# Squares of queries and keys in two fp32r parts: the sum over a head as two products with ones, behind the next tile's third quarter

## The chip, the cores and the metric

The kernel runs on one core of one Trainium2 chip. The metric is the device time in microseconds, lower is better. The engines are TensorE (PE, products), VectorE (DVE), ScalarE (ACT), GpSimd (POOL) and SyncE (SP, which starts transfers). Each works through its own queue in order, and they wait for one another by counting semaphores.

## The reference, cut to what matters

One layer of a hybrid encoder on 512 tokens of width 2048 in fp32: a combined input projection, three branches (banded attention, an RG-LRU, cross-attention into a memory), a gated merge, and a product-key expert layer. The change touches one spot: every query and key head of the banded attention is normed by the root mean square over its 128 numbers.

```
def rms_norm(x, g):
    y = xf * lax.rsqrt(jnp.mean(xf * xf, axis=-1, keepdims=True) + EPS)
    return (y * g.astype(jnp.float32)).astype(x.dtype)
...
h = rms_norm(x, norm1_g)
qa, ka, va, xl, gl, qc = jnp.split(h @ w_in, cuts, axis=-1)
qa = rms_norm(qa.reshape(B, S, A_HEADS, A_HEAD_DIM), attn_q_norm_g)
ka = rms_norm(ka.reshape(B, S, A_HEADS, A_HEAD_DIM), attn_k_norm_g)
...
log_a = -LRU_C * r * jax.nn.softplus(-lam)
a = jnp.exp(log_a)
mult = jnp.sqrt(jnp.clip(1.0 - jnp.exp(2.0 * log_a), 1e-12, 1.0))
u = mult * (i * xc)          # then an associative scan over the tokens
```

## The kernel before, in words

Activations lie transposed, features on the 128 partitions and the 512 tokens along the free axis. A weight tile is 2048x128 (16 blocks of 128x128); with it TensorE makes 128 output features for all tokens in one PSUM bank. fp32r is a form of fp32 with fewer bits that TensorE takes in one pass. To keep precision each product is made of three fp32r products (`split_mm`): high by high, high by low, low by high. The high part of a tile (`p_hi`) is a rounding copy on ScalarE (`high_part`), the low part (`p_lo`) a subtraction on POOL (`low_part`), and the two stand in single buffers that are refilled by quarters of four blocks: as soon as TensorE has used a quarter of one tile, that quarter of the next is rounded and subtracted. A tile is 48 products, a quarter is 12.

The stretch of the change is the sixteen tiles of queries and keys: loop `t` from 0 to 3 and `k` from 0 to 3, head 4t+k, tile into `bank[k]`. For each head, when its tile is done:

- ScalarE copies the bank to the arena, writes its square to `sq[k % 2]`, refills `p_hi`, and later takes the square root of the sum (`head_root`, which waits for `head_ss`).
- TensorE sums the square over the 128 partitions by one fp32 product with a 128x128 matrix of ones (`head_sum`, into bank 4 or 5). It does so in the middle of the *next* head's tile, behind its first quarter (`between` in `project_split`, `last_head`). The last head's product stands in the first tile of the values.
- VectorE takes the reciprocal of the root and scales the head (`head_norm`: a RECIPROCAL at L1218 and a SCALAR_TENSOR_TENSOR at L1220).

Written into the same loops is part of the RG-LRU branch. For t = 0 TensorE makes gate products behind the ones product, and ScalarE the sigmoids and tanh (`gate_pair`). For t = 1 VectorE computes the factors behind each head's norm (`lru_factors`, L1279 to L1285, seven instructions of 128x512, one of them a RECIPROCAL). For t = 2 ScalarE takes a root and VectorE does the scan (`lru_scan`, three instructions). All queues are written by hand; there is no scheduler. Buffers for the squares and roots are double, so ScalarE waits for the ones product of head k-2 before it writes a square, and for the norm of head k-2 before it writes a root.

Of the kernel before, what the change touches and what calls it, by code (L numbers as in the profile page):

```python
# [158 lines left out]
def hybrid_block(nc, x_t, mem_t, g1, g2, gmem, head_g, w_memk, w_memv, w_qk, w_lru_in, w_v, rel_rev,  # L159
                 lru_w, lru_vec, w_mix, b_gate, w_o, w_pq, keys, w_exp, u_rows, v_rows, out_t):  # L160
    ctx = ExitStack()
    with ctx:
# [109 lines left out]
        ig = at(XL, LC, S)  # L272
        la = at(Z + 2048, LC, S)
        lr = at(TZ + 1536, S)
        fill_sq = [place(f"fill_sq{i}", 199.0625 + 2 * i, [S]) for i in range(2)]

        tb = at(TZ, HA, 2 * P)
# [115 lines left out]
        wg_in, act_raw = [sem(f"wg_in{i}") for i in range(2)], [sem(f"act_raw{i}") for i in range(2)]  # L393
        u_gelu, act_part, act_ok, y_added = sem("u_gelu"), sem("act_part"), sem("act_ok"), sem("y_added")
        out_done = sem("out_done")
        wait_held, pool_held = sem("wait_held"), sem("pool_held")
        dve_step, pool_step = sem("dve_step"), sem("pool_step")

        def band_s(e, q):
# [222 lines left out]
        def _(pool):  # L622
# [126 lines left out]
            def gather(first, rows, index, t, following=None):  # L749
                for b in range(4):  # L750

                    pool.wait_ge(gath_col, 4 * t + b + 1 + first)
                    for half in range(2):
                        to = 2 * (b % 2) + half
                        pool.wait_ge(gath_free, 8 * t + 2 * b + half + 1 + 2 * first)  # L755
                        pool.sem_inc(pool_held, 1)
                        pool.indirect_dma_start(grow[to][:, :], None, rows,  # L757
                                                bass.IndirectOffsetOnAxis(g_col[b][:, half:half + 1], 0)).then_inc(gath_in[to], 16)
                    if following is None or b < 2:
                        column(index, 4 * t + b + 2, (b + 2) % 4)  # L760
                    else:
                        column(following, b - 2, b - 2)
# [26 lines left out]
        def _(act_e):  # L789
# [107 lines left out]
            for t in range(N_QK // 4):  # L897
                for k in range(4):
                    act_e.wait_ge(tile_done, 4 * t + T_QK + k + 1)
                    f(head_place(t, k), bank[k][:, :]).then_inc(acc_copied, 1)  # L900
                    act_e.wait_ge(head_ss, 4 * t + k + HC - 1)
                    f(sq[k % 2], bank[k][:, :], ACT.Square).then_inc(head_sq, 1)
                    ahead = (k % 2, 4 * t + S_QK + k + 2, 2 * t + S_QK // 2 + k // 2 + 2, 4 * t + T_QK + k + 2)
                    high_part(*ahead, quarters=(0,))
                    act_e.wait_ge(head_ok, 4 * t + k + HC - 1)
                    head_root(k, S, 4 * t + k + HC + 1)
                    if t == 0:
                        gate_pair(k)
                    if t == 2:
                        act_e.wait_ge(lru_m2, k + 1)  # L910
                        f(rg[:, k, :], rg[:, k, :], ACT.Sqrt).then_inc(lru_mult, 1)
                    high_part(*ahead, quarters=(1, 2, 3))

            act_e.wait_ge(lru_ok, LC)
            act_e.wait_ge(rel_out, 16)
# [263 lines left out]
        def _(dve):  # L1179
# [107 lines left out]
            def lru_scan(k):  # L1287
# [5 lines left out]
                v.tensor_tensor_scan(out=gl[:, k, :], data0=la[:, k, :], data1=u, initial=0.0, op0=ALU.mult, op1=ALU.add  # L1293
                                     ).then_inc(lru_ok, 1)

            dve.wait_ge(conv_ok, LC)

            for t in range(N_QK // 4):
                for k in range(4):
                    head_norm(k, head_place(t, k), S, hgain[:, t // 2:t // 2 + 1], 4 * t + k + HC + 1)  # L1300
                    if t == 1:
                        lru_factors(k)
                    if t == 2:
                        lru_scan(k)
# [159 lines left out]
            def best16(groups):  # L1464

                def pause():
                    st.wait()
                    dve.sem_inc(wait_held, 1)

                dve.sem_inc(wait_held, 1)  # L1470
                for half in (slice(0, 8), slice(8, 16)):
                    for s, val, idx in groups:
                        st.did(v.max(val[:, half], s))
                    pause()
                    for s, val, idx in groups:
                        st.did(v.max_index(idx[:, half], val[:, half], s))
                    pause()
                    if half.start == 0:
                        for s, val, idx in groups:
                            st.did(v.match_replace(s, val[:, half], s, LOWEST))  # L1480
                        pause()
# [282 lines left out]
        def _(pe):  # L1764
# [60 lines left out]
            def project_split(number, out, r_hi, r_lo, between=None):  # L1825

                for q in range(4):
                    pe.wait_ge(quarter_lo, 4 * number + q + 1)
                    for c in range(4 * q, 4 * q + 4):
                        ins = split_mm(out, p_hi[:, c, :], p_lo[:, c, :], r_hi[:, c, :], r_lo[:, c, :], c == 0, c == KC - 1)  # L1830
                    ins.then_inc(part_used if q < 3 else tile_done, 1)
                    if q == 0 and between is not None:
                        between()


# [19 lines left out]
            def last_head(t, k):  # L1855

                pe.wait_ge(head_rt, 4 * t + k + HC - 2)
                head_sum((k - 1) % 4, S, 4 * t + k + HC)

            def with_gates(t, k):  # L1860
                if t or k:
# [17 lines left out]
            for half in range(2):  # L1879
                if half:  # L1880
                    pe.wait_ge(head_rt, HC + N_QK)
                for n in range(4):
                    wh, wl = (w[:, :, :].rearrange("p (c a) b -> p c (a b)", c=4) for w in (p_hi, p_lo))
                    for c in range(4):
# [5 lines left out]
                            ins = split_mm(bank[4 * half + m][:, :], norm_hi[:, 4 * n + c, tok], norm_lo[:, 4 * n + c, tok],  # L1890
                                           wh[:, c, :], wl[:, c, :], n == 0 and c == 0, n == 3 and c == 3)
                        ins.then_inc(part_used if c < 3 else tile_done, 1)
                        if half == 0 and n == 0 and c == 0:
                            last_head(N_QK // 4, 0)


# [374 lines left out]
```

## Time and profile before

| | us |
|---|---|
| median of 3 runs | 3813.01 (3811.71 to 3814.02) |
| the profiled execution's own time | 3809.69 |
| its span | 3807.9 |
| TensorE busy | 3759.3 (99%) |
| VectorE busy | 2364.7 (62%) |
| ScalarE busy | 1262.9 (33%) |
| POOL busy | 1702.0 (45%) |

Matmuls overlap in the records: one fp32r product of 512 columns is recorded with 0.39 us, while the next starts 0.23 us later. So the cost of a product is read from the distance of the starts, not from its duration. An fp32 product appears as two records (x2). In a timeline the bracket at the end of a row tells how long the engine was idle before it and who ended that.

### The profile page before, as it was taken

Reading aid. Unit: us, or ns where it says so; the run is one execution under the profiler, and the core shown is the slowest. Engines: PE = TensorE matmul, PEld = TensorE weight load, DVE = VectorE, ACT = ScalarE, POOL = GpSimd, SP = SyncE. Lnnn points to the kernel's source line nnn. Section 1 sums busy time; section 2 is a strip of 40 time slices with the busy share of each in tenths; the row PEclk is TensorE's granted clock in tenths of the full one; section 3 lists DMA queues with packets and bytes.
Section 4 is the critical chain, followed back from the end, with each engine's and each line's share of the span. In section 5 each row is a group of like instructions: output and inputs, shape, how many; then the busy total and the mean of one; then the engine's idle time right before and its main releaser. Section 6 shows DMA issues by size and latency. Waiting matters only on the chain. (4 is left out here: it accounts for less than half of the span.)

```text
span 3807.9 us, 56597 instructions
## 1 busy us (share of the span) xinstructions
PE 3759.3 (99%) x20173; PEld 3446.9 (91%) x20173; DVE 2364.7 (62%) x4027; ACT 1262.9 (33%) x1638; POOL 1702.0 (45%) x1449
## 2 busy tenths in 40 slices
PE   7999999999999998999999999999999999999999
PEld 5778778888888887889999999999999999999999
DVE  5482453000010207886968888888887888888887
ACT  3433453333333323224652222222222222222221
POOL 0444334444444662444015555545553655554223
PEclk9999999999999999999999999999999999999999
DMA  6222112222222322334569998899987898889787
GB/s 205 92 88 100 67 58 98 99 92 95 99 99 92 140 99 104 105 105 151 211 247 330 326 332 318 322 326 334 322 313 281 319 339 311 316 320 340 275 295 249
DMA packets 187946, 800.97 MB, mean 210 GB/s; under 512 B 21024, under 2 KB 59944, under 8 KB 134440
## 3 DMA queue, kind: packets, MB, share of 16 engines
q1 hardware_dynamic: 99776, 492.34, 35.8%
q0 software_dynamic: 83872, 303.22, 22.4%
q10 hardware_dynamic: 4184, 4.01, 0.5%
q8 instruction: 56, 0.92, 0.1%
q14 instruction: 58, 0.48, 0.0%
HBM read 762.39 MB, written 37.09 MB: 210 GB/s over the span
## 5 line engine op out<-in xcount | busy, mean ns | idle before, releaser
L791 ACT ACTIVATE w_hi<-ring 128x1024 fp32r<-128x1024 f32 (+1 forms) x499 | 564.0, 1135 | 1090.1 <-PE bank L1766 718.8
L637 POOL TENSOR_TENSOR p_lo<-ring,p_hi 128x512 fp32r<-128x512 f32 x432 | 563.9, 1306 | 672.5 <-ACT p_hi L791 672.5
L1766 PE MATMUL bank<-h_hi,w_hi 128*128 128x368 f32 (+1 forms) x2304 | 780.3, 339 | 13.1 <-DVE h_lo L1449 7.3
L1766 PE MATMUL bank<-h_lo,w_hi 128*128 128x368 f32 (+1 forms) x2304 | 773.9, 336 | 0.0
L1766 PE MATMUL bank<-h_hi,w_lo 128*128 128x368 f32 (+1 forms) x2304 | 773.7, 336 | 0.0
L1766 PE MATMUL bank<-act_hi,w_hi 128*128 128x368 f32 x2048 | 673.1, 329 | 0.3 <-DVE xT L1640 0.3
L1766 PE MATMUL bank<-act_hi,w_lo 128*128 128x368 f32 x2048 | 672.8, 329 | 0.0
L1766 PE MATMUL bank<-act_lo,w_hi 128*128 128x368 f32 x2048 | 672.8, 328 | 0.0
L757 POOL DMA_INDIRECT grow<-v_rows,g_col x288 | 382.2, 1327 | 516.3 <-DVE g_acc L1621 389.9
L1586 DVE TENSOR_TENSOR w_lo<-ring,w_hi 128x1024 fp32r<-128x1024 f32 x448 | 546.2, 1220 | 77.3 <-ACT w_hi L791 56.6
L791 ACT ACTIVATE p_hi<-ring 128x512 fp32r<-128x512 f32 x464 | 292.7, 632 | 788.7 <-PE bank L1766 784.2
L757 POOL DMA_INDIRECT grow<-u_rows,g_col x288 | 376.0, 1305 | 387.1 <-DVE grow L1614 308.1
L1766 PE MATMUL bank<-norm_hi,p_hi 128*128 128x512 f32 x1216 | 487.0, 400 | 1.7 <-POOL p_lo L637 1.7
L1766 PE MATMUL bank<-norm_hi,p_lo 128*128 128x512 f32 x1216 | 473.7, 390 | 0.0
L1766 PE MATMUL bank<-norm_lo,p_hi 128*128 128x512 f32 x1216 | 473.3, 389 | 0.0
L1766 PEld LDWEIGHTS bank<-h_hi,w_hi 128*128 128x128 f32 x2304 | 433.6, 188 | 25.7 <-issue 8.7
L1766 PEld LDWEIGHTS bank<-h_lo,w_hi 128*128 128x128 f32 x2304 | 433.6, 188 | 9.8
L1766 PEld LDWEIGHTS bank<-h_hi,w_lo 128*128 128x128 f32 x2304 | 433.2, 188 | 10.2
L1393 DVE TENSOR_TENSOR arena<-arena,bank 128x512 f32<-128x512 f32 x48 | 30.1, 683 | 572.4 <-PE bank L1766 572.4
L1766 PEld LDWEIGHTS bank<-act_hi,w_hi 128*128 128x128 f32 x2048 | 384.1, 188 | 1.2 <-DVE xT L1640 1.2
L1766 PEld LDWEIGHTS bank<-act_lo,w_hi 128*128 128x128 f32 x2048 | 384.1, 188 | 0.0
L1766 PEld LDWEIGHTS bank<-act_hi,w_lo 128*128 128x128 f32 x2048 | 384.1, 188 | 0.0
(219 smaller groups left out, 5056.3 us busy)
## 6 DMA issues: line engine op xcount, KB each, us to landing
ring<-w_exp SPq DMA_DIRECT2D x256, 1024.0 KB
ring<-w_mix SPq DMA_DIRECT2D x64, 1024.0 KB, 4.9
tables<-wt SPq DMA_DIRECT2D x12, 2048.0 KB, 6.8
wg<-tables SPq DMA_DIRECT2D x96, 256.0 KB
ring<-w_qk SPq DMA_DIRECT2D x20, 1024.0 KB, 4.9
ring<-w_o SPq DMA_DIRECT2D x16, 1024.0 KB, 4.9
ring<-w_pq SPq DMA_DIRECT2D x16, 1024.0 KB
xT<-x_t SPq DMA_DIRECT2D x8, 1024.0 KB, 11.9
```

What stands on the lines that cost most here:

```text
L637: nc.gpsimd.tensor_tensor(p_lo[:, part, :], ring[slot][:, part, :], p_hi[:, part, :].bitcast(F32), ALU.subtract).then_inc(quarter_lo, 1)
L757: pool.indirect_dma_start(grow[to][:, :], None, rows, bass.IndirectOffsetOnAxis(g_col[b][:, half:half + 1], 0)).then_inc(gath_in[to], 16)
L791: return nc.scalar.activation(out, in_, func, **kw)
L1393: v.tensor_tensor(sig[:, b, :], sig[:, b, :], bank[3 + b][:, :], ALU.mult).then_inc(y_used, 1)
L1586: v.tensor_tensor(w_lo[b][:, part, :], ring[b][:, part, :], w_hi[b][:, part, :].bitcast(F32), ALU.subtract).then_inc(split_lo, 1)
L1766: return nc.tensor.matmul(out, lhsT, rhs, start=start, stop=stop)
```

## The change: what it does

- ScalarE rounds each square once more, to `sq_hi` (fp32r); VectorE subtracts it from the square, to `sq_lo` (fp32r), which lies where the square lay. `ones_r` is an fp32r copy of the ones, made once.
- TensorE's fp32 ones product of a head becomes two fp32r products into the same bank, ones by `sq_hi` and ones by `sq_lo`. They wait for a new counter, `head_lo`, that VectorE raises with each subtraction, instead of for ScalarE's square.
- The products (with the gate products where there are any) stand behind the third quarter of the next tile instead of behind its first; on ScalarE the root and what follows it stand behind the next tile's third p_hi quarter.
- The subtraction stands at the head of a head's round on VectorE, before its norm.
- Two counters that only mark held instructions become one.

```diff
@@ ScalarE
                     f(sq[k % 2], bank[k][:, :], ACT.Square).then_inc(head_sq, 1)
+                    act_e.wait_ge(head_sq, 4 * t + k + HC + 1)
+                    f(sq_hi[k % 2][:, :], sq[k % 2]).then_inc(h_high, 1)
                     ahead = (k % 2, 4 * t + S_QK + k + 2, 2 * t + S_QK // 2 + k // 2 + 2, 4 * t + T_QK + k + 2)
-                    high_part(*ahead, quarters=(0,))
+                    high_part(*ahead, quarters=(0, 1, 2))
                     act_e.wait_ge(head_ok, 4 * t + k + HC - 1)
                     head_root(k, S, 4 * t + k + HC + 1)
...
-                    high_part(*ahead, quarters=(1, 2, 3))
+                    high_part(*ahead, quarters=(3,))
@@ VectorE
+            v.tensor_copy(ones_r[:, :], ones[:, :]).then_inc(head_lo, 1)
             dve.wait_ge(conv_ok, LC)

             for t in range(N_QK // 4):
                 for k in range(4):
+                    dve.wait_ge(h_high, KC + 4 * t + k + 1)
+                    v.tensor_tensor(sq_lo[k % 2][:, :], sq[k % 2], sq_hi[k % 2][:, :].bitcast(F32), ALU.subtract
+                                    ).then_inc(head_lo, 1)
                     head_norm(k, head_place(t, k), S, hgain[:, t // 2:t // 2 + 1], 4 * t + k + HC + 1)
@@ TensorE
-                    if q == 0 and between is not None:
+                    if q == 2 and between is not None:
                         between()
...
             def last_head(t, k):

                 pe.wait_ge(head_rt, 4 * t + k + HC - 2)
-                head_sum((k - 1) % 4, S, 4 * t + k + HC)
+                n = (k - 1) % 2
+                pe.wait_ge(head_lo, 4 * t + k + 1)
+                mm(bank[4 + n][:, :], ones_r[:, :], sq_hi[n][:, :], start=True, stop=False)
+                mm(bank[4 + n][:, :], ones_r[:, :], sq_lo[n][:, :], start=False, stop=True).then_inc(head_ss, 1)
...
-                        if half == 0 and n == 0 and c == 0:
+                        if half == 0 and n == 0 and c == 2:
                             last_head(N_QK // 4, 0)
```

How the instructions stand in the queues is shown at two places; the code lines of the changed kernel lie a few lines lower. First VectorE's queue before, from the norm of head 4 (t = 1, k = 0; `hgain` is the head's gain, `head_rt` counts ScalarE's roots) through the RG-LRU factors to the norm of head 5:

```order
L1218 RECIPROCAL arena<-arena 128x512 [waits head_rt]
L1220 SCALAR_TENSOR_TENSOR arena<-arena,hgain 128x512 [waits dve_step]
L1279 TENSOR_SCALAR arena<-arena 128x512 [waits lru_tanh]
L1280 RECIPROCAL arena<-arena 128x512 [waits dve_step]
L1281 TENSOR_SCALAR arena<-arena 128x512 [waits dve_step]
L1282 TENSOR_TENSOR arena<-arena 128x512 [waits dve_step]
L1283 SCALAR_TENSOR_TENSOR arena<-arena 128x512 [waits dve_step]
L1284 TENSOR_TENSOR arena<-arena 128x512 [waits dve_step]
L1285 TENSOR_SCALAR arena<-arena 128x512 [waits dve_step]
L1218 RECIPROCAL arena<-arena 128x512 [waits head_rt]
```

And the same stretch of it now, where `sq_hi_121` and `sq_lo_123` are the two parts of head 5's square:

```order
L1225 RECIPROCAL arena<-arena 128x512 [waits head_rt]
L1227 SCALAR_TENSOR_TENSOR arena<-arena,hgain 128x512 [waits dve_step]
L1286 TENSOR_SCALAR arena<-arena 128x512 [waits lru_tanh]
L1287 RECIPROCAL arena<-arena 128x512 [waits dve_step]
L1288 TENSOR_SCALAR arena<-arena 128x512 [waits dve_step]
L1289 TENSOR_TENSOR arena<-arena 128x512 [waits dve_step]
L1290 SCALAR_TENSOR_TENSOR arena<-arena 128x512 [waits dve_step]
L1291 TENSOR_TENSOR arena<-arena 128x512 [waits dve_step]
L1292 TENSOR_SCALAR arena<-arena 128x512 [waits dve_step]
L1309 TENSOR_TENSOR sq_lo_123<-arena,sq_hi_121 128x512 [waits h_high]
L1225 RECIPROCAL arena<-arena 128x512 [waits head_rt]
```

The subtraction of head 5 stands behind the norm and the factors of head 4, and ahead of head 5's own norm.

Next ScalarE's queue before, in the round of a head of t = 1 (copy, square, then `p_hi` by quarters, with the root in between, which alone reads `eps`):

```order
L791 ACTIVATE arena<-bank 128x512 [waits tile_done]
L791 ACTIVATE arena<-bank 128x512 [waits head_ss]
L791 ACTIVATE p_hi<-ring_52 128x512 [waits part_used,pair_in1]
L791 ACTIVATE arena<-bank,eps 128x512 [waits head_ss,head_ok]
L791 ACTIVATE p_hi<-ring_52 128x512 [waits part_used,pair_in1]
L791 ACTIVATE p_hi<-ring_52 128x512 [waits part_used]
L791 ACTIVATE p_hi<-ring_52 128x512 [waits tile_done]
```

And now:

```order
L796 ACTIVATE arena<-bank 128x512 [waits tile_done]
L796 ACTIVATE arena<-bank 128x512 [waits head_ss]
L796 ACTIVATE sq_hi_121<-arena 128x512 [waits head_sq]
L796 ACTIVATE p_hi<-ring_52 128x512 [waits part_used,pair_in1]
L796 ACTIVATE p_hi<-ring_52 128x512 [waits part_used] x2
L796 ACTIVATE arena<-bank,eps 128x512 [waits head_ss,head_ok]
L796 ACTIVATE p_hi<-ring_52 128x512 [waits tile_done,pair_in1]
```

The root has moved behind two more quarters of p_hi, and the rounding of the square is new, ahead of them all.

## Rows read from the trace of the kernel before

**Rows 1.** The page's first part: busy us, share of the span, instructions.
```profile
PE 3759.3 (99%) x20173; PEld 3446.9 (91%) x20173; DVE 2364.7 (62%) x4027; ACT 1262.9 (33%) x1638; POOL 1702.0 (45%) x1449
```

**Rows 2.** Windows: busy us (instructions) of PE, PEld, DVE, ACT, POOL; PEclk, DMA share, GB/s.
```profile
200.00:240.00 40.00, 40.00 (x171) 31.86 (x170) 36.84 (x27) 15.39 (x25) 17.95 (x14) 1.00 0.29 105
240.00:280.00 40.00, 40.00 (x173) 32.01 (x172) 38.17 (x25) 15.50 (x27) 18.80 (x15) 1.00 0.22 79
320.00:360.00 40.00, 40.00 (x176) 32.73 (x176) 8.55 (x5) 10.58 (x18) 18.10 (x14) 1.00 0.33 115
```

**Rows 3.** Waits of PE from 60 to 620 us: total us, times, longest us.
```profile
PE bank L1766 <- POOL p_lo L637: 1.7, 1, 1.7
...
```

**Rows 4.** Timeline of PE: start us, us, engine, instruction, count.
```profile
293.57 1.02 PE L1766 MATMUL bank<-arena,ones 128*128 128x512 f32 x2
...
294.65 0.39 PE L1766 MATMUL bank<-norm_lo,p_hi 128*128 128x512 f32 x1
...
305.35 1.02 PE L1766 MATMUL bank<-arena,ones 128*128 128x512 f32 x2
```

**Rows 5.** Timeline of ACT: heads 1 and 12, same columns.
```profile
159.99 1.28 ACT L791 ACT_TABLE_LOAD   x1 [0.21 <-PE bank L1766]
...
165.67 0.62 ACT L791 ACTIVATE p_hi<-ring 128x512 fp32r<-128x512 f32 x1
...
294.68 0.69 ACT L791 ACTIVATE arena<-bank,eps 128x512 f32<-128x512 f32 x1 [0.23 <-PE bank L1766]
```

**Rows 6.** Timeline of DVE in the head tiles.
```profile
202.44 3.35 DVE L1218 RECIPROCAL arena<-arena 128x512 f32<-128x512 f32 x1 [8.47 <-ACT arena L791]
...
212.36 1.68 DVE L1284 TENSOR_TENSOR arena<-arena 128x512 f32<-128x512 f32 x1
...
214.41 3.35 DVE L1218 RECIPROCAL arena<-arena 128x512 f32<-128x512 f32 x1
...
223.87 1.83 DVE L1282 TENSOR_TENSOR arena<-arena 128x512 f32<-128x512 f32 x1
...
227.52 3.35 DVE L1218 RECIPROCAL arena<-arena 128x512 f32<-128x512 f32 x1
...
240.75 3.34 DVE L1218 RECIPROCAL arena<-arena 128x512 f32<-128x512 f32 x1
...
253.68 3.35 DVE L1218 RECIPROCAL arena<-arena 128x512 f32<-128x512 f32 x1
...
261.75 3.32 DVE L1218 RECIPROCAL arena<-arena 128x512 f32<-128x512 f32 x1
...
271.84 3.35 DVE L1218 RECIPROCAL arena<-arena 128x512 f32<-128x512 f32 x1 [1.27 <-ACT arena L791]
...
295.40 3.35 DVE L1218 RECIPROCAL arena<-arena 128x512 f32<-128x512 f32 x1 [3.63 <-ACT arena L791]
```

**Rows 7.** Timeline of POOL in the head tiles.
```profile
212.07 1.41 POOL L637 TENSOR_TENSOR p_lo<-ring,p_hi 128x512 fp32r<-128x512 f32 x1 [1.48 <-ACT p_hi L791]
...
223.85 1.29 POOL L637 TENSOR_TENSOR p_lo<-ring,p_hi 128x512 fp32r<-128x512 f32 x1 [1.48 <-ACT p_hi L791]
```

**Rows 8.** Two tiles, norm_hi and norm_lo: ns min/median/max, first and last start.
```profile
L791 ACT ACTIVATE norm_hi<-hT x16: 629/630/634, 62.9 to 81.4; 128x512 fp32r<-128x512 f32 x16
```
...
L1242 DVE TENSOR_TENSOR norm_lo<-hT,norm_hi x16: 671/674/693, 63.6 to 82.0; 128x512 fp32r<-128x512 f32 x16
```

**Rows 9.** Timeline of DVE and PE behind the merge: h_lo, and the product behind it.
```profile
1448.62 0.69 DVE L1449 TENSOR_TENSOR h_lo<-arena,h_hi 128x512 fp32r<-128x512 f32 x1
...
1449.45 0.76 PE L1766 MATMUL bank<-h_hi,w_hi 128*128 128x512 f32 x1 [7.29 <-DVE h_lo L1449]
```

**Rows 10.** Windows near the start (columns as in rows 2), and PE's timeline.
```profile
22.00:23.00 1.00, 0.00 (x0) 0.00 (x0) 0.96 (x3) 1.00 (x2) 0.00 (x0) 0.76 1.02 397
...
25.00:26.00 1.00, 1.00 (x4) 0.82 (x3) 1.00 (x3) 1.00 (x2) 0.00 (x0) 0.54 1.04 422
...
23.07 1.19 PE L1766 MATMUL bank<-arena,ring 128*128 128x256 f32 x2 [4.38 <-DVE arena L1202]
```

More of the change, by code:

```diff
@@ L274, in hybrid_block @@
         lr = at(TZ + 1536, S)
+        sq_hi = [nc.alloc_sbuf_tensor_at(f"sq_hi{i}", [P, S], F32R, offset=base + 96 * 1024 + 4 * (QC + 512 * i))
+                 for i in range(2)]
+        sq_lo = [nc.alloc_sbuf_tensor_at(f"sq_lo{i}", [P, S], F32R, offset=base + 96 * 1024 + 4 * (Z + 1024 * i + 512))
+                 for i in range(2)]
+        ones_r = place("ones_r", 203.0625, [P], F32R)
         fill_sq = [place(f"fill_sq{i}", 199.0625 + 2 * i, [S]) for i in range(2)]
@@ L395, in hybrid_block @@
         out_done = sem("out_done")
-        wait_held, pool_held = sem("wait_held"), sem("pool_held")
+        held, head_lo = sem("held"), sem("head_lo")
         dve_step, pool_step = sem("dve_step"), sem("pool_step")
@@ L755, in gather @@
                         pool.wait_ge(gath_free, 8 * t + 2 * b + half + 1 + 2 * first)
-                        pool.sem_inc(pool_held, 1)
+                        pool.sem_inc(held, 1)
                         pool.indirect_dma_start(grow[to][:, :], None, rows,
@@ L1467, in pause @@
                     st.wait()
-                    dve.sem_inc(wait_held, 1)
-                dve.sem_inc(wait_held, 1)
+                    dve.sem_inc(held, 1)
+                dve.sem_inc(held, 1)
                 for half in (slice(0, 8), slice(8, 16)):
```

## The prediction

> **What bounds the kernel now.** I read the page's busy times first: TensorE is busy 99% of the span [rows 1]. The reader is to see that little but TensorE work or a TensorE wait can move the end. Then the stretch that the change touches, the 16 head tiles from about 134 to 329 us, by windows [rows 2]: TensorE shows no idle time and its clock is granted in full, but VectorE is busy 36.8 and 38.2 of 40 us between 200 and 280 us, against 8.6 of 40 later. That second figure is the one to keep. The waits of TensorE from 60 to 620 us [rows 3] are three, of which the longest is 1.7 us: its queue runs from product to product, and nothing in the stretch is there to be won back but the products themselves. Last I read the timelines of the engines for single rounds.
>
> **What the ones products cost and what replaces them.** In a late tile [rows 4] the ordinary products go from 294.65 to 305.35 us in 47 steps, 0.2277 us each. From the start of the fp32 ones product (293.57) to 294.65 lie that product and one ordinary one: 1.08 - 0.23 = 0.85 us. From one ones product to the next is 11.78 us, the round of a head. The change puts two fp32r products of 512 columns there, which the stream prices at 2 x 0.2277 = 0.455 us. Gain 0.40 us a head, 16 heads: -6.4 us. Bounds: if each new product cost its whole record of 0.39 us, only 0.07 us a head would go (-1.1 us); if the second, which has the same weights as the first, cost next to nothing, 0.63 us (-10 us). I take -6.4, since the stream around it consists of such products. A round without waits becomes 11.38 us.
>
> **What is added beside TensorE.** ScalarE gets 16 roundings of 0.63 us [rows 8]; it is busy 15.5 of 40 us, so they cost nothing. In the first four heads it also does root, gates and table loads, which now come behind the third quarter: from the load at 159.99 to the next p_hi at 165.67 are 5.7 us [rows 5], after which the fourth quarter's p_hi (0.63) and p_lo (1.3) follow. The load starts 0.7 us after the ones product does, the tile ends 4.9 us after it (0.455, two fp32 gate products of 0.85, a quarter of 2.73), so this p_lo is ready 3.5 us into the next tile, which wants it after three quarters (8.2 us). Covered by 4.7 us; beyond that it would cost the excess, four times. The last tile's product goes behind the third quarter of the first V tile, and the last head's norm comes 5 us later; POOL asks for it many V tiles on. The merged counter of held indirect loads and the single copy of the ones cost nothing that I can see. The quarters of p_hi that are moved ahead of the root have no row that waits for the root.
>
> **The term that decides: the low part stands in VectorE's queue.** Each head gets a subtraction of 128x512 with fp32r output, 0.67 us alone [rows 8]. It stands at the head of the next round, so *behind* the norm and the RG-LRU factors of the head before. And TensorE now waits for it (head_lo); before it waited only for ScalarE's square. So in heads 4 to 7 a closed loop arises: ones product of head k-1, root, reciprocal, norm, seven factor instructions, subtraction of head k, ones product of head k. Its length, from rows:
> - ones product to root 1.11 us, root to reciprocal 0.72 us [rows 4 to 6]; less the 0.40 that the product is shorter: 1.43.
> - reciprocal to reciprocal through norm and factors: the first begins at 202.44, the fifth at 253.68, none of the five waiting in between [rows 6]: 51.24 / 4 = 12.81.
> - subtraction: 0.72 with its gap; it reads two operands in the arena beside POOL's p_lo and can be held as other such instructions are. L1284 took 1.68 instead of some 0.7 us with a p_lo begun at 212.07, L1282 1.83 with one begun at 223.85 [rows 6, 7]. The round of 11.97 us has one such case of 0.99 and a small one of 0.10, so the bare round is 10.88, and the mean holds 1.93 us of collisions over seven exposed instructions, 0.28 each. Subtraction 1.0.
> - from VectorE's end to TensorE's start 0.14 (1449.31 to 1449.45) [rows 9].
>
> Sum 15.4 us against a round of 11.38: TensorE stands 4.0 us, before the products of heads 5, 6, 7 and 8, each time anew, since the loop starts from the delayed product. Behind the waiting product stand the fourth quarter of its tile and everything that follows on TensorE. 4 x 4.0 = +16.0 us. The first loop has a table load (1.28, as at 159.99) ahead of its root; part of it is lost against a p_lo that would hold the same instruction anyway: +0.6.
>
> Bounds of a stall: without any collision 1.43 + 10.88 + 0.72 + 0.14 - 11.38 = 1.8 us; with the worst round seen (13.23, from four rounds) and a held subtraction (1.83) 5.2 us. So +7.2 to +21 for the four.
>
> The Trainium skill (SBUF — State Buffer, section "SBUF: two separate sides") says that VectorE and GpSimd hold their shared port pair exclusively for a whole instruction, a VectorE instruction with two SBUF inputs included, and that the other fully blocks. The rows of 1.68 and 1.83 us beside a p_lo agree. By that rule the collisions stay in the loop, 4.0 us a stall; if the ports were merely split evenly, the stall would lie nearer to 1.8 us.
>
> In heads 8 to 11 the three scan instructions stand in the loop instead: reciprocal to reciprocal 8.07 us at 253.68 to 261.75, and 8.8 us (10.09 less 1.27 idle) at 261.75 to 271.84 [rows 6]. With 1.43, 0.72 to 1.83 and 0.14 the loop is 10.4 to 12.2 against 11.38: 0 to 0.8 us a head; I take +0.2 in all. In the other eight heads it is 1.43 + 4.1 + 1.0 and never decides.
>
> **The clock.** After 4.38 us of idle before 23.07 us the granted clock was 0.76 in the window 22 to 23 and 0.50 until 25 to 26 (0.54) [rows 10]: it fell to the level of 1.2 GHz some 4.1 us after TensorE's last product and cost about 1.4 us (2.9 us at half speed). A stall of 4.0 us lies just at that edge. A fall in a stall whose loop follows costs only the longer ones product (0.45 us), for the loop is otherwise made of VectorE work and the slower tile merely shortens the next stall; only behind the last stall would the 1.4 us count in full. Between 0 and 3.2 us; I take +0.7.
> The Trainium skill (TensorE: Matmul & The Clock Gate, section "What's actually happening") has it that throttled is the default state and only activity releases it; were all four stalls long enough, its rule would give the full 3.2 us, which makes rival 3.
>
> **Sum.** -6.4 + 16.0 + 0.6 + 0.2 + 0.7 = +11.1 us. Against the profiled execution's 3809.7 us (span 3807.9 and 1.8 around it) that is 3820.8; the median of the runs is 3813.0, 3.3 higher, and the change adds the same to it: **3824**. The delay passes through whole: later stages start from TensorE's queue.
>
> **Rivals.**
> 1. *No stall (3806.6).* The place is the product of head 5. If the subtraction were done by then, only the -6.4 us would stand. It decides from where the loop is under 11.38 us. For it: TensorE was never held by VectorE here before [rows 3]. Against it: the bare loop of 13.2 us is longer, and rounds of VectorE alone took 12.81 us. Chance 4%.
> 2. *Short stalls (3814 to 3819).* The pause of TensorE also pauses ScalarE and POOL, so fewer p_lo fall on factor instructions; with stalls of 1.8 to 2.8 us the sum is -6.4 + 7.2 to 11.2, or +0.8 to +4.8, and with a little clock and scan up to +6. For it: between two stalls POOL makes four p_lo in 15.4 instead of 11.78 us. Against it: each p_lo follows its tile quarter at a fixed distance, so the same instructions are hit every round. 14%.
> 3. *Long stalls and a fallen clock (3830 to 3837).* Stalls near 5.2 us, or the clock down after each, scan rounds held: -6.4 + 21 + 3.2 + 2, at most +20; from about +17 on I count it here. For it: the 4.1 us edge. Against it: a fall shortens the following stall. 12%.
> 4. *Faster by over 0.2% (3805 and less).* Needs no stall and the cheap second product, -10 us. 1%.
>
> The forecast itself, 3819 to 3830, has 69%.
>
> **How the numbers follow.** A measurement tells about 0.2%, 7.6 us, from no change. Faster: 1 to 2%. Within 0.2% (3805.4 to 3820.6): rivals 1 and 2 and the low edge of the forecast, 0.04 + 0.14 + 0.02 = 0.20. Slower: the rest, 0.78. Range for 8 in 10: 3815.5 to 3831, which leaves out rival 1, the lower end of 2 and the upper half of 3; both ends are of one sign.
>
> **What would show it.** In the profile after: TensorE waits for the subtraction's line four times, some 4 us each, longest between 205 and 270 us, and nowhere else in the head tiles; two ones products with 0.23 us steps; rounds of 11.38 us in heads 12 to 15 and of 15.4 us in heads 5 to 8; VectorE without idle time in heads 4 to 7; the granted clock at or just below full there. I am wrong if TensorE has no wait there, if ScalarE's fourth-quarter p_hi is late in heads 0 to 3 (TensorE waiting for p_lo), or if the time lost is seen in a stage behind the head tiles.

## The result, and the profile after

| | before | after |
|---|---|---|
| median of 7 runs, us | 3811.89 (3808.34 to 3814.04) | 3824.83 (3819.64 to 3827.48) |
| ratio, 95% interval | | 1.0027 [1.0018, 1.0036] |
| span of the profiled execution | 3807.9 | 3824.1 |
| head 0's ones product to the first product behind the merge | 1298.6 | 1308.7 |

By the ratio the changed kernel is slower by 10.3 us (6.9 to 13.7); the medians lie 12.9 us apart. The last line of the table is the measure that I use throughout, and I call it the stretch: it is read from one trace and holds no noise of the later gathers. It begins with head 0's ones product, behind the third quarter of the next tile. In the kernel before that product stands behind the first quarter, at 145.41 us, so its stretch is counted from two quarters later, 24 steps of 0.2277 us: from 150.87 to 1449.45 [rows 9]. After, it runs from 151.23 to 1459.97: +10.1 us, so the whole loss was made before the merge, and the waits below put it into the head tiles. The two spans differ by 16.2; of the rest, 3.8 us are waits of TensorE for the low part of a weight tile behind gathers (7.6 against 3.8 us from 1470 us on), a thing that varies from run to run (3.1 us in e5, 9.7 in e7); the last 2 us I have not traced.

Busy times of the page, against rows 1. TensorE is busy as long as before in a longer span:

```profile
PE 3759.9 (98%) x20173; PEld 3451.9 (90%) x20173; DVE 2374.5 (62%) x4044; ACT 1272.4 (33%) x1654; POOL 1701.2 (44%) x1449
```

The windows of rows 2 again (PE, PEld, DVE, ACT, POOL busy; granted clock; DMA):

```profile
200.00:240.00 40.00, 34.74 (x141) 27.87 (x140) 29.24 (x22) 14.73 (x24) 15.40 (x12) 0.91 0.20 75
240.00:280.00 40.00, 34.77 (x142) 27.94 (x141) 32.97 (x26) 13.55 (x23) 15.74 (x12) 0.91 0.24 79
320.00:360.00 40.00, 40.00 (x177) 32.92 (x176) 15.37 (x9) 14.15 (x24) 18.12 (x14) 1.00 0.33 113
```

TensorE now has 10.5 us without work in 80, and the clock is not full. VectorE, the engine that is waited for, is *less* busy there than before (29.2 and 33.0 against 36.8 and 38.2 us). An engine in a closed loop waits itself for a part of each round; its busy share does not show that it is the bound. The waits do. TensorE's, 60 to 620 us (total us, times, longest), against rows 3:

```profile
PE bank L1777 <- DVE sq_lo L1309: 10.5, 4, 4.0
PE bank L1777 <- POOL p_lo L642: 1.7, 1, 1.7
```

Four waits, all for the subtraction. The products of heads 4 to 9 on TensorE's timeline, with those of 12 (against rows 4):

```profile
203.55 0.40 PE L1777 MATMUL bank<-sq_hi,ones_r 128*128 128x512 f32 x1
203.78 0.39 PE L1777 MATMUL bank<-sq_lo,ones_r 128*128 128x512 f32 x1
...
219.06 0.77 PE L1777 MATMUL bank<-sq_hi,ones_r 128*128 128x512 f32 x1 [3.96 <-DVE sq_lo L1309]
...
234.55 0.47 PE L1777 MATMUL bank<-sq_hi,ones_r 128*128 128x512 f32 x1 [1.30 <-DVE sq_lo L1309]
...
250.11 0.77 PE L1777 MATMUL bank<-sq_hi,ones_r 128*128 128x512 f32 x1 [3.93 <-DVE sq_lo L1309]
...
265.43 0.47 PE L1777 MATMUL bank<-sq_hi,ones_r 128*128 128x512 f32 x1 [1.30 <-DVE sq_lo L1309]
...
276.85 0.40 PE L1777 MATMUL bank<-sq_hi,ones_r 128*128 128x512 f32 x1
...
311.03 0.40 PE L1777 MATMUL bank<-sq_hi,ones_r 128*128 128x512 f32 x1
```

From start to start: 15.51, 15.49, 15.56, 15.32 us, then 11.42 and on to 311.03 in three rounds of 11.39. The waits alternate, 3.96 and 1.30, but the rounds do not: behind a long wait the clock is down, the tile's products take longer, and the next wait is shorter by that much. So the loss is not the waits (10.5 us) but what the four rounds are longer: 61.88 against 4 x 11.39 = 45.56, or 16.3 us.

The loop in VectorE's timeline, head 4's norm to head 5's:

```profile
206.41 3.35 DVE L1225 RECIPROCAL arena<-arena 128x512 f32<-128x512 f32 x1 [7.50 <-ACT arena L796]
...
216.22 1.63 DVE L1291 TENSOR_TENSOR arena<-arena 128x512 f32<-128x512 f32 x1
217.89 0.43 DVE L1292 TENSOR_SCALAR arena<-arena 128x512 f32<-128x512 f32 x1
218.23 0.68 DVE L1309 TENSOR_TENSOR sq_lo<-arena,sq_hi 128x512 fp32r<-128x512 f32 x1
221.07 3.35 DVE L1225 RECIPROCAL arena<-arena 128x512 f32<-128x512 f32 x1 [2.16 <-ACT arena L796]
```

The subtraction ends at 218.91 and TensorE starts at 219.06. VectorE then waits 2.16 us for the root that hangs on this very product: that idle bracket is the closed loop. L1291 took 1.63 us beside the p_lo that began at 215.84, as L1284 did before [rows 6].

And the clock, by windows of 1 us (columns as in rows 2):

```profile
217.00:218.00 1.00, 0.00 (x0) 0.00 (x0) 0.96 (x2) 0.00 (x0) 0.31 (x1) 0.88 0.00 0
218.00:219.00 1.00, 0.00 (x0) 0.00 (x0) 0.91 (x2) 0.00 (x0) 0.00 (x0) 0.50 0.00 0
...
223.00:224.00 1.00, 1.00 (x4) 0.77 (x3) 1.00 (x1) 0.00 (x0) 0.00 (x0) 0.50 0.00 0
224.00:225.00 1.00, 1.00 (x5) 0.82 (x4) 0.96 (x2) 0.00 (x0) 0.00 (x0) 0.70 0.00 0
```

TensorE's last product before the wait ended at 215.10. The clock fell at about 217.8 to the 1.2 GHz level and came back at about 224.6, so 5.5 us of work ran at half speed; behind the second long wait it was 5.2.

### The profile page after: what moved, and what is told of

It is laid out like the page before. It is cut to its first block, busy times and chain, and to the rows that moved or that the text cites. A ratio compares the mean times of both kernels' runs of the same rounds, so it can differ in the third digit from the quotient of the medians.

```text
span 3824.1 us, 56630 instructions
## 1 busy us (share of the span) xinstructions
PE 3759.9 (98%) x20173; PEld 3451.9 (90%) x20173; DVE 2374.5 (62%) x4044; ACT 1272.4 (33%) x1654; POOL 1701.2 (44%) x1449
## 4 chain that ended last, share of the span: by engine, by line
PE 85%; issue 7%; DMA 3%; DVE 3%; POOL 1%; ACT 1%; ACTq 0%; POOLq 0%; DVEq 0%
PE bank L1777 85%; DMA grow<-v_rows,g_col 2%; DMA grow<-u_rows,g_col 1%; POOL grow L762 1%; DVE arena L1287 0%; DVE arena L1225 0%; DVE w_lo L1597 0%; DVE g_acc L1632 0%; PE bank L1939 0%; ACT w_hi L796 0%; POOL g_col L752 0%; DVE arena L1291 0%; ACT arena L796 0%; POOL w_lo L733 0%; DVE xT L1651 0%
## 5 line engine op out<-in xcount | busy, mean ns | idle before, releaser
L796 ACT ACTIVATE w_hi<-ring 128x1024 fp32r<-128x1024 f32 (+1 forms) x499 | 564.2, 1136 | 1113.4 <-PE bank L1777 711.9
L642 POOL TENSOR_TENSOR p_lo<-ring,p_hi 128x512 fp32r<-128x512 f32 x432 | 566.0, 1311 | 681.0 <-ACT p_hi L796 681.0
L1777 PE MATMUL bank<-h_hi,w_hi 128*128 128x368 f32 (+1 forms) x2304 | 781.5, 339 | 17.1 <-DVE w_lo L1597 7.6
L1777 PE MATMUL bank<-h_lo,w_hi 128*128 128x368 f32 (+1 forms) x2304 | 775.4, 337 | 0.0
L1777 PE MATMUL bank<-h_hi,w_lo 128*128 128x368 f32 (+1 forms) x2304 | 775.0, 336 | 0.0
L1777 PE MATMUL bank<-act_hi,w_hi 128*128 128x368 f32 x2048 | 672.8, 328 | 0.0
L1777 PE MATMUL bank<-act_lo,w_hi 128*128 128x368 f32 x2048 | 672.8, 328 | 0.0
L1777 PE MATMUL bank<-act_hi,w_lo 128*128 128x368 f32 x2048 | 672.8, 328 | 0.0
L796 ACT ACTIVATE p_hi<-ring 128x512 fp32r<-128x512 f32 x464 | 292.6, 632 | 780.7 <-PE bank L1777 776.4
L1777 PE MATMUL bank<-norm_hi,p_hi 128*128 128x512 f32 x1216 | 484.2, 398 | 1.7 <-POOL p_lo L642 1.7
L1777 PE MATMUL bank<-norm_hi,p_lo 128*128 128x512 f32 x1216 | 475.1, 391 | 0.0
L1777 PE MATMUL bank<-norm_lo,p_hi 128*128 128x512 f32 x1216 | 475.0, 391 | 0.0
L1777 PEld LDWEIGHTS bank<-h_hi,w_hi 128*128 128x128 f32 x2304 | 434.6, 189 | 29.8 <-DVE w_lo L1597 9.0
L1777 PEld LDWEIGHTS bank<-h_hi,w_lo 128*128 128x128 f32 x2304 | 434.3, 188 | 10.2
L1777 PEld LDWEIGHTS bank<-h_lo,w_hi 128*128 128x128 f32 x2304 | 434.6, 189 | 9.9
L1777 PEld LDWEIGHTS bank<-act_hi,w_hi 128*128 128x128 f32 x2048 | 384.1, 188 | 0.0
L1777 PEld LDWEIGHTS bank<-act_lo,w_hi 128*128 128x128 f32 x2048 | 384.1, 188 | 0.0
L1777 PEld LDWEIGHTS bank<-act_hi,w_lo 128*128 128x128 f32 x2048 | 384.1, 188 | 0.0
```

What stands on the lines that cost most here:

```text
L642: nc.gpsimd.tensor_tensor(p_lo[:, part, :], ring[slot][:, part, :], p_hi[:, part, :].bitcast(F32), ALU.subtract).then_inc(quarter_lo, 1)
L796: return nc.scalar.activation(out, in_, func, **kw)
L1777: return nc.tensor.matmul(out, lhsT, rhs, start=start, stop=stop)
```

## The experiments

"Stretch" is the last line of the table above, against 1298.6 us before; for e5 it starts two quarters behind the beginning of its first wait. Ratios are to the kernel before on the same chip.

| kernel | stretch | ratio, 95% interval |
|---|---|---|
| after | +10.1 | 1.0027 [1.0018, 1.0036] |
| e1_pool_sub | -6.2 | 0.9975 [0.9963, 0.9987] |
| e2_high_only | -10.2 | 0.9978 [0.9969, 0.9987] |
| e3_square_wait | 0.0 | 1.0002 [0.9993, 1.0012] |
| e4_no_recip | -2.0 | 0.9995 [0.9986, 1.0004] |
| e5_first_quarter | +17.1 | 1.0044 [1.0031, 1.0057] |
| e6_place_only | 0.0 | 1.0006 [0.9997, 1.0015] |
| e7_sub_first | +4.4 | 1.0013 [1.0004, 1.0021] |
| e8_more_recip | +22.7 | 1.0064 [1.0052, 1.0076] |
| e9_keep_busy | +10.3 | 1.0030 [1.0021, 1.0040] |

The theory is the closed loop; the rivals are that the added work, the new place, a low part wherever it is made, or the fallen clock costs the time.

### e1: the subtraction on POOL

```diff
@@ VectorE
-                    dve.wait_ge(h_high, KC + 4 * t + k + 1)
-                    v.tensor_tensor(sq_lo[k % 2][:, :], sq[k % 2], sq_hi[k % 2][:, :].bitcast(F32), ALU.subtract
-                                    ).then_inc(head_lo, 1)
@@ POOL, behind low_part of tile `number` (the tile ahead)
+                pool.wait_ge(h_high, KC + number - S_QK)
+                nc.gpsimd.tensor_tensor(sq_lo[n][:, :], sq[n], sq_hi[n][:, :].bitcast(F32), ALU.subtract
+                                        ).then_inc(head_lo, 1)
```

> The subtraction of each square's low part is done by POOL, behind the fourth p_lo quarter of the tile ahead, instead of standing in VectorE's queue; all else as in the changed kernel. Theory (the loop through VectorE's factors holds TensorE): TensorE waits nowhere in the head tiles, rounds are 11.4 us from head 4 on, and only the shorter products are left: 6.4 us under the kernel before, ratio 0.9983 (3805.5 us where before has 3812). VectorE's rounds with factors go back to about 12.8 us. Rival (any product that waits for a low part is late, wherever it is made, or the fp32r pair and its place cost the time): ratio 1.002 to 1.003, TensorE still held four times. Rival (POOL becomes the late one): TensorE waits for p_lo or for the subtraction by up to 1 us a head, ratio 0.999 to 1.002.

TensorE has no wait for a low part of a square left; these are its waits from 60 to 620 us, two products of the former loop, and POOL's subtraction for head 8:

```profile
PE bank L1795 <- POOL p_lo L642: 1.7, 1, 1.7
PE bank L1795 <- DVE arena L1361: 1.6, 1, 1.6
PE bank L1795 <- DVE mix_lo_c L1415: 0.2, 1, 0.2
```

```profile
215.14 0.40 PE L1795 MATMUL bank<-sq_hi,ones_r 128*128 128x512 f32 x1
...
226.53 0.40 PE L1795 MATMUL bank<-sq_hi,ones_r 128*128 128x512 f32 x1
```

```profile
243.76 1.29 POOL L650 TENSOR_TENSOR sq_lo<-arena,sq_hi 128x512 fp32r<-128x512 f32 x1 [0.34 <-ACT sq_hi L817]
245.01 1.47 POOL L642 TENSOR_TENSOR p_lo<-ring,p_hi 128x512 fp32r<-128x512 f32 x1
```

Rounds are 11.39 us from head 4 on. POOL's next p_lo begins where the subtraction ends, and TensorE waits for neither. The stretch is 6.2 us shorter than before. This is also the version that beats both kernels, by its interval 5 to 14 us under the one before. One expectation missed: VectorE's rounds did not go back to 12.8 us, they take 14.3 ((263.85 - 206.61) / 4), because POOL now has a fifth instruction a head that can hold VectorE: an instruction of 0.69 us (L1312) took 1.67 at 233.04, beside the POOL subtraction of a square that began at 232.42. Nobody waits for these rounds.

### e2: the high part alone

```diff
-                pe.wait_ge(head_lo, 4 * t + k + 1)
-                mm(bank[4 + n][:, :], ones_r[:, :], sq_hi[n][:, :], start=True, stop=False)
-                mm(bank[4 + n][:, :], ones_r[:, :], sq_lo[n][:, :], start=False, stop=True).then_inc(head_ss, 1)
+                pe.wait_ge(head_lo, 1)
+                pe.wait_ge(h_high, KC + 4 * t + k)
+                mm(bank[4 + n][:, :], ones_r[:, :], sq_hi[n][:, :]).then_inc(head_ss, 1)
```
(and the subtraction removed)

> The low part is left out: one fp32r product of ones by the rounded square, which waits for ScalarE's rounding alone (the sums lose the low parts). Theory: no wait in the head tiles, and 0.855 less 0.228 us a head are saved, 16 heads: 10.0 us under the kernel before, ratio 0.9974. If a fp32r product of ones costs more than the step of the stream around it, the ratio lies between 0.9974 and 0.9983. Rival (rounding on ScalarE or the later place costs the 10 to 12 us): ratio 1.001 or more.

Stretch -10.2, rounds of 11.13 us (214.87 to 226.00), no wait for a square. The price list holds to a few hundredths: beside 48 steps of 0.2277 us (10.93) the round of 11.78 leaves 0.85 us for the fp32 product, that of 11.13 leaves 0.20 for one fp32r product, and that of 11.39 leaves 0.46 for two. The ratio's interval (0.9969 to 0.9987) includes 0.9974.

### e3: all the work, without the wait

```diff
-                pe.wait_ge(head_lo, 4 * t + k + 1)
-                mm(bank[4 + n][:, :], ones_r[:, :], sq_hi[n][:, :], start=True, stop=False)
-                mm(bank[4 + n][:, :], ones_r[:, :], sq_lo[n][:, :], start=False, stop=True).then_inc(head_ss, 1)
+                head_sum((k - 1) % 4, S, 4 * t + k + HC)
@@ sq_lo in a buffer of its own; ScalarE, before the square
+                    if 4 * t + k > 1:
+                        act_e.wait_ge(head_lo, 4 * t + k)
```

> All the added work and the new places stay (rounding, subtraction at the head of VectorE's round, third quarter), but TensorE does the old fp32 product on the square and waits for ScalarE's square alone; the low part is made beside it and read by nobody. Theory (the wait is what costs, not the work): no wait in the head tiles, rounds of 11.78 us, ratio 1.0000 +- 0.0005; VectorE's rounds with factors 13.5 to 14 us, and nobody waits for them. Rival (the added VectorE or ScalarE work or the later root costs): ratio 1.002 to 1.003 with TensorE waiting for p_lo or a root.

Stretch 0.0. VectorE has the same subtraction in the same place, and gets later with each head, but TensorE waits for the square alone:

```profile
221.09 0.69 DVE L1311 TENSOR_TENSOR sq_lo<-arena,sq_hi 128x512 fp32r<-128x512 f32 x1
...
235.65 0.68 DVE L1311 TENSOR_TENSOR sq_lo<-arena,sq_hi 128x512 fp32r<-128x512 f32 x1
...
250.15 0.68 DVE L1311 TENSOR_TENSOR sq_lo<-arena,sq_hi 128x512 fp32r<-128x512 f32 x1
```

14.5 us a round, where 13.5 to 14 had been expected, against 11.78 of TensorE. TensorE is not held by it: the work costs nothing, only the wait for it does.

### e4: a shorter loop, and e8: a longer one

```diff
@@ e4, lru_factors
-                step(v.reciprocal(lr, lr))
@@ e8, lru_factors
                 step(v.reciprocal(lr, lr))
+                step(v.reciprocal(spare_r, rt[k % 2]))
```

> The changed kernel, with the reciprocal left out of the RG-LRU factors (that output is computed otherwise). It takes 3.39 us out of the loop of heads 4 to 7, nothing else. Theory: the loop of 15.5 us becomes 12.1 (11.5 to 13 with other collisions with p_lo), against 11.4: four waits of 0.1 to 1.6 us instead of 3.96, 1.30, 3.93, 1.30, granted clock 1.00 throughout the head tiles, and the time 0.4 to 6 us under the kernel before (ratio 0.9985 to 1.0000). Rival (the four waits come from the subtraction itself or from ScalarE, not from the length of the factors): ratio stays 1.0027.

> The changed kernel with one more reciprocal of 128x512 in the factors of heads 4 to 7, into a buffer that nobody reads: the suspected cost made larger by 3.4 us a head. Theory: each of the four loops grows by 3.4 us (15.5 to 18.9) and all of it reaches the end: 13.6 us above the changed kernel, ratio 1.0063 (1.0053 to 1.0072), four waits between 3 and 7.5 us, of which the alternate ones are short where the clock fell. Rival (the waits have slack in them and absorb a part): ratio 1.003 to 1.005.

TensorE's waits in e4, and in e8:

```profile
PE bank L1776 <- DVE sq_lo L1308: 3.4, 4, 1.6
```

```profile
PE bank L1779 <- DVE sq_lo L1311: 20.8, 4, 6.4
```

In e4, which leaves the reciprocal of the factors out, the first loop is 13.13 us (204.06 to 217.19), the next three 12.20, 12.20 and 12.25, and the clock stays at 1.00. Against the changed kernel the four loops are 12.1 us shorter, 13.6 by count (3.39 us in each). In e8 they are 17.96, 18.06, 18.76 and 18.04, together 10.9 us longer and not 13.6, since VectorE's instructions were held less by p_lo: 3.5 us in the four loops, against 6.7 in the changed kernel and 9.1 in e4. The stretch of e8 still moves by +12.5 us, because of the round behind the loops:

```profile
277.08 0.47 PE L1779 MATMUL bank<-sq_hi,ones_r 128*128 128x512 f32 x1 [4.20 <-DVE sq_lo L1311]
...
290.12 0.40 PE L1779 MATMUL bank<-sq_hi,ones_r 128*128 128x512 f32 x1
```

```profile
277.00:278.00 1.00, 0.92 (x3) 0.81 (x4) 0.00 (x0) 0.03 (x1) 0.00 (x0) 0.77 0.00 0
278.00:279.00 1.00, 1.00 (x4) 0.71 (x4) 0.31 (x1) 1.00 (x2) 0.00 (x0) 0.50 0.00 0
```

The clock fell behind the last wait, and this round took 13.04 us without a wait, where 11.42 stood: 1.6 us. So the ratio of e8 is the expected one partly by luck: each loop, given 3.39 us more of work, became 2.4 to 3.2 us longer, and the clock, which had no term in this forecast, made up for more than half of the rest. The rival (ratio 1.003 to 1.005) is excluded by the interval; what the loops did not pass on went into fewer collisions and not into slack in the waits.

### e5: behind the first quarter, and e6: the place alone

```diff
@@ e5, on the changed kernel
-                    if q == 2 and between is not None:
+                    if q == 0 and between is not None:
-                    high_part(*ahead, quarters=(0, 1, 2))
+                    high_part(*ahead, quarters=(0,))
@@ e6, on the kernel before
-                    if q == 0 and between is not None:
+                    if q == 2 and between is not None:
-                    high_part(*ahead, quarters=(0,))
+                    high_part(*ahead, quarters=(0, 1, 2))
```
(the last head's place and ScalarE's remaining quarters with them)

> The two fp32r products as in the changed kernel, but behind the next tile's first quarter, where the fp32 product stood, and ScalarE's order as before. Theory: the loop of heads 4 to 7 does not contain the place, so the four waits stay (about 16 us before the clock's share, as in the changed kernel), and in the other twelve heads the low part comes too late for a first quarter: copy, square, rounding and subtraction end about 3.3 us behind the tile, the quarter lasts 2.7, so about 0.6 us a head more. Together 7 us above the changed kernel: ratio 1.0046 (1.0035 to 1.0060). Rival (the third quarter is what costs): ratio 0.998 to 1.000. Rival (place without effect): 1.0027.

> The kernel before, with its one fp32 product and the root moved behind the third quarter, nothing else. Theory: no wait anywhere, rounds of 11.78 us, ratio 1.0000 (0.9995 to 1.0005). Rival (the later root delays p_hi in the heads with gates, or the later norm delays the attention): 1.0005 to 1.002, with TensorE waiting for p_lo or behind the head tiles.

e5's waits, and a product outside the loop:

```profile
PE bank L1777 <- DVE sq_lo L1309: 15.9, 16, 3.9
```

```profile
275.93 0.47 PE L1777 MATMUL bank<-sq_hi,ones_r 128*128 128x512 f32 x1 [0.46 <-DVE sq_lo L1309]
```

Sixteen waits instead of four: those of the loop as before (3.92, 1.25, 3.93, 1.24; loops of 15.52, 14.50, 15.52 and 15.36 us), and 0.46 us in each other head (0.53 in the first), whose rounds are 12.04 to 12.09 us instead of 11.39, and 13.77 to 13.80 instead of 13.08 where gate products stand in them. So the third quarter is right for the two-part product; it is no cause of the loss. e6 confirms it from the other side: the stretch is unchanged, rounds are 11.78 us, and TensorE has the three waits of rows 3 and no other. Its ratio of 1.0006 lies just above the expected 1.0005, with an interval that reaches from 0.9997 to 1.0015.

### e7: the subtraction ahead of the factors

```diff
@@ VectorE, per head: norm, subtraction of the next head, factors
-                    dve.wait_ge(h_high, KC + 4 * t + k + 1)
-                    v.tensor_tensor(sq_lo[k % 2][:, :], ...).then_inc(head_lo, 1)
                     head_norm(k, ...)
+                    if 4 * t + k + 1 < N_QK:
+                        square_low(4 * t + k + 1)
                     if t == 1:
                         lru_factors(k)
```

> The changed kernel, but VectorE subtracts the low part of head k+1 between the norm of head k and its factors, so the factors no longer stand ahead of it. Theory: the closed loop is gone, but VectorE's rounds with factors, norm and subtraction take 14.5 us against 11.4, so it falls 3.1 us further behind with each of four heads, and from the third on the subtraction is late for want of time: waits of about 1, 3 and 3 us at heads 7, 8 and 9, none before. Sum -6.4 + 7 = +0.8 us, ratio 1.0002 (0.9990 to 1.0008), clearly below the changed kernel's 1.0027. Rival (any subtraction on VectorE is late by 4 us in each of the four heads): 1.0027. Rival (order alone was the fault and VectorE has time enough): 0.9983.

```profile
227.27 0.47 PE L1784 MATMUL bank<-sq_hi,ones_r 128*128 128x512 f32 x1 [0.44 <-DVE sq_lo L1307]
...
241.76 0.47 PE L1784 MATMUL bank<-sq_hi,ones_r 128*128 128x512 f32 x1 [2.86 <-DVE sq_lo L1307]
...
255.31 0.47 PE L1784 MATMUL bank<-sq_hi,ones_r 128*128 128x512 f32 x1 [0.30 <-DVE sq_lo L1307]
...
269.80 0.77 PE L1784 MATMUL bank<-sq_hi,ones_r 128*128 128x512 f32 x1 [2.90 <-DVE sq_lo L1307]
```

The kind was foreseen, the size was too small, and the ratio of 1.0013 lies above the expected range, though its interval reaches into it. Head 5 has no wait, and it begins at head 6, not 7. Here the subtraction falls on a p_lo from head 6 to 9 (1.75 to 1.78 us instead of 0.68), and VectorE starts 1.3 us later for the table load, so it runs out of time a head sooner. The rounds of heads 6 to 10 are 11.99, 14.49, 13.55, 14.49 and 12.96 us, together 10.5 above 11.39; less 6.2 is the +4.4 of the stretch. I had expected 7 for the 10.5. The new order alone gives back 5.7 us of the 16.3; for the rest, VectorE has no time for one more instruction a head while it does the factors, and 1.6 of the 10.5 us are the clock: the last of these rounds shows a fall with nothing behind it to absorb it, 12.96 us without any wait.

### e9: TensorE kept busy through the waits

```diff
+                if not hold_off(t, k):
+                    for _ in range(12):
+                        mm(bank[4 + n][:, :], norm_hi[:, 0, 0:P], norm_hi[:, 0, :])
                 pe.wait_ge(head_lo, 4 * t + k + 1)
```
(and TensorE's tiles of heads 8 to 11 written out instead of looped)

> The changed kernel, with twelve fp32r products of 512 columns into the same bank ahead of the wait for the low part in heads 5 to 8 (2.7 us each, overwritten by the real ones): TensorE works through most of the 3.9 us in which it otherwise stands. What is asked is whether the clock that fell behind the waits cost time. Theory (the loop is made of VectorE's work, a slow tile only shortens the next wait): waits of about 1 us, granted clock 1.00 throughout, loops of 15.0 to 15.6 us as before, ratio 1.0022 to 1.0028, at most 2 us under the changed kernel. Rival (the two falls, 5.3 us at half speed each, are lost time): 5 us under the changed kernel, ratio 1.0014. Rival (added work adds up): ratio 1.0050.

```profile
220.40 0.50 PE L1777 MATMUL bank<-sq_hi,ones_r 128*128 128x512 f32 x1 [1.18 <-DVE sq_lo L1309]
...
235.90 0.50 PE L1777 MATMUL bank<-sq_hi,ones_r 128*128 128x512 f32 x1 [1.15 <-DVE sq_lo L1309]
...
251.41 0.50 PE L1777 MATMUL bank<-sq_hi,ones_r 128*128 128x512 f32 x1 [1.15 <-DVE sq_lo L1309]
...
266.92 0.50 PE L1777 MATMUL bank<-sq_hi,ones_r 128*128 128x512 f32 x1 [1.15 <-DVE sq_lo L1309]
```

```profile
221.96 3.35 DVE L1225 RECIPROCAL arena<-arena 128x512 f32<-128x512 f32 x1 [1.61 <-ACT arena L796]
...
235.16 0.68 DVE L1309 TENSOR_TENSOR sq_lo<-arena,sq_hi 128x512 fp32r<-128x512 f32 x1
```

The granted clock is 1.00 in every window from 200 to 280 us, and from the product at 204.95 to that at 266.92 are 61.97 us, against 61.88 in the changed kernel. Neither the 10.9 us of added products nor the missing fall of the clock moved the sum of the loops. Inside them two things moved against each other: from product to reciprocal it is 1.56 us here (220.40 to 221.96), where the changed kernel has 2.01 at the lower clock, and from reciprocal to the end of the subtraction 13.88 us, where it has 13.33. The ratio of 1.0030 lies above the expected 1.0022 to 1.0028, but by less than its uncertainty; the stretch of +10.3 us, 1.0027, lies in it.

## Why the prediction was right

Forecast 3824 us, measured 3824.83. The mechanism held: a closed loop, in the four rounds named, of the length named. That the two times agree to 0.8 us is luck: the median before came out 1.1 us lower here than the one that the forecast started from, the runs of one kernel spread by 6 to 8 us, and several terms below were off in opposite directions.

- *The product.* Foreseen 0.40 us a head. Measured 0.39: rounds of 11.39 for 11.78, and 13.08 for 13.48 in the heads with gates. e2 and e1 confirm both prices. Shown.
- *The closed loop.* Foreseen 15.4 us, measured 15.3 to 15.6, at the four heads named. That the wait is the cause, and not the work, the place or the clock, is shown by e3, e6 and e9; that the length of the loop sets the loss, by e4 and e8; that it is VectorE's queue, by e1. A microsecond of work is not a microsecond of the loop, though: what is added or taken away shifts the collisions with p_lo (e4 passed on 12.1 of 13.6 us, the loops of e8 10.9).
- *Its parts.* Two errors cancelled. Ones product to reciprocal took 2.86 us in the first loop, with the table load, then 2.01 (219.06 to 221.07, at the lower clock), 1.52 (234.55 to 236.07) and 2.01: 2.10 in the mean, not 1.43 and a share of the 0.6. The first of the two products carries a start of 0.31 us behind a wait, and the lower clock nearly 0.5. Reciprocal to the end of the subtraction took 12.50, 13.33, 13.90 and 13.16 us, mean 13.2, where I had 13.8: the subtraction was never held (0.68 or 0.69 each time), because the last p_lo had ended before it or the next began behind it (233.72 and 233.99). The 0.28 us that I gave each exposed instruction was an average from a queue that ran freely against POOL. In the loop L1291 was hit four times of four, L1288 three times (0.43, 1.23, 1.36, 1.05 us), L1227 once (1.21) and the subtraction never. In e7, where it stands elsewhere, it is hit in each of heads 6 to 9.
- *The collisions.* I took it that POOL's subtraction holds a VectorE instruction for its whole length. 1.63 to 1.67 us for L1291 in all four loops agree with that. Rival 2, short stalls, rested on fewer hits: they did become fewer, 1.7 us a loop where I had 2.2, and what that gave was taken back between product and reciprocal.
- *The waits.* I wrote four waits of some 4 us as the sign; they came as 3.96, 1.30, 3.93 and 1.30, since a fallen clock shortened every second one, which the part on the clock had foreseen. The sign "VectorE without idle time in heads 4 to 7" was wrong: VectorE waited 2.16, 1.67 and 2.16 us for the roots at heads 5 to 7, and the loop as I had added it up already held 1.43 us in which it can only wait.
- *The table load* ahead of the first root, +0.6: measured 0.0. The load made the way to the reciprocal 1.3 us longer, but the first loop, 15.51 us, is as long as the others: its way from reciprocal to subtraction is the 12.50 us one, with one collision instead of two or three. That the load's shift is why is likely and not shown.
- *The scan rounds*, +0.2: measured 0.0 (11.42 and 11.39 us).
- *The clock*, +0.7: right in its argument, mis-sized in its parts. It fell twice, 2.7 and 2.3 us after the last product, where I had read 4.1 (in rows 10 a mean of 0.76 from 22 to 23 us puts the fall at 22.5, which is 3.8 behind the product), and more than 5 us of work ran slowly each time, where I had reckoned 2.9. The slow tile came off the next wait, as argued. What a fall adds to a loop is the 0.5 us between product and reciprocal, where I had 0.45. In e9, without a fall, that is gone, but VectorE's four ways from reciprocal to subtraction are 1.3 us longer in sum (54.2 against 52.9), so the loops are as long as before; no run parts the two effects. No fall lay behind the last wait here. Where one did, in e7 and e8, it cost 1.6 us, near the 1.4 that I had.
- *ScalarE's cover* in heads 0 to 3: foreseen p_lo 3.5 us into the next tile; POOL's began at 158.46 and took 1.29, so it ended 3.6 us behind the tile's end. TensorE never waited for it.

Sum by measured parts: -6.2 + 16.3 = +10.1 us, where the forecast had +11.1.

## What to carry to other kernels

A cheaper instruction that waits for a new operand is priced by where the *maker* of that operand stands in its queue. Go once around: if the maker stands behind work that itself hangs on the previous one of the cheap instructions, the sum of that round is a floor for the period, and what exceeds the old period is paid each time; work that was late but unwaited-for before costs nothing until somebody waits for it. The cure that worked here was to move the maker to an engine whose queue had a gap at that point (e1). A faster maker would not have done it: the subtraction is 0.7 us of a loop that is 4.1 us too long. The price of such a loop can't be had from mean instruction times alone, since what stands in it decides anew which instructions collide with another engine's.

## What the runs showed of the hardware that was not expected

- How long TensorE had been idle when the granted clock fell differed from case to case: 2.7 us (last product ended 215.10, fell 217.8) and 2.3 us in the changed kernel, 3.7, 4.3 and 3.7 us in e8. In three runs it also fell when a wait was over and work had begun again: in e7 behind one of 2.86 us (windows from 242 to 246 us: 0.67, 0.50, 0.50, 0.63), in e8 behind 4.20 us, in e5 behind 3.92 us. It did not fall in e4, whose longest wait was 1.57 us, nor behind the waits of 1.30. The time at the lower level was 3.4 us in e7 and 6.8 in the changed kernel; e5 and e8 have both.
- In a closed loop a fallen clock mostly moves idle time: waits of 3.96, 1.30, 3.93, 1.30 us for rounds of 15.51, 15.49, 15.56, 15.32. Behind the last wait it counts: 1.6 us in e7 and in e8.
- Which VectorE instruction is held by POOL depends on its place against p_lo and not on a chance per instruction: the same subtraction took 0.68 us four times of four behind the factors, and 1.75 to 1.78 four times of four beside p_lo in e7. For others the place drifts from loop to loop, as for L1288 above.
- Not every instruction is held alike. The scan took 2.2 us in all its four rounds of the changed kernel, begun each time while a p_lo was in progress (the first beside the one that began at 272.38), and 1.22 to 1.23 us in those of e7, begun while none was. The reciprocals took 3.32 to 3.35 us in either case. The first scan of the changed kernel, and the first of e7:

```profile
272.86 2.20 DVE L1300 TENSOR_TENSOR_SCAN arena<-arena 128x512 f32<-128x512 f32 x1
```

```profile
271.02 1.22 DVE L1300 TENSOR_TENSOR_SCAN arena<-arena 128x512 f32<-128x512 f32 x1
```
